# A mixture-of-experts kernel on one core: the matrix of routing weights made by VectorE from lists along the free axis

## The reference

```python
lg = (hf @ w_rg + b_rg)                       # 8 group logits per token
grp = jnp.argmax(lg, axis=-1)                 # one group of 8
le_sel = ...                                  # the 8 expert logits of that group
top_v, top_j = lax.top_k(le_sel, 2)           # two experts of it
wts = pg_top * jax.nn.softmax(top_v, axis=-1)
...
def expert_block(args):
    xb, e = args
    return (jax.nn.silu(xb @ w_g[e]) * (xb @ w_u[e])) @ w_d[e]
...
yb = yb * row_w[:, None]
out = jnp.zeros((N, D)).at[row_tok].add(yb)
```

## Time and profile before

| | us |
|---|---|
| median of 3 runs | 1274.16 (1273.81 to 1274.68) |
| the profiled execution | 1274.61 |
| its span, first to last instruction | 1272.5 |
| PE busy | 1164.9 (92%) |
| VectorE busy | 465.5 (37%) |
| ScalarE busy | 311.8 (25%) |
| HBM read | 406.22 MB, 321 GB/s over the span |

### The profile page before, as it was taken

How to read it: one execution, slowest core, us unless ns; L and a number is a source line. 1 busy time by engine, 2 the same in 40 slices (tenths; PEclk the granted TensorE clock), 3 DMA queues, 4 the chain that set the end, 5 groups by cost and what they waited for, 6 DMA issues and landing times.

```text
span 1272.5 us, 34338 instructions
## 1 busy us (share of the span) xinstructions
PE 1164.9 (92%) x14651; PEld 737.1 (58%) x14652; DVE 465.5 (37%) x1045; ACT 311.8 (25%) x752; POOL 142.9 (11%) x84
## 2 busy tenths in 40 slices
PE   5999999989998998789999999999999978897786
PEld 4878777768874554445555555555555544454443
DVE  3799443444344232132233333223332212322123
ACT  4133234384221121111122111112211211121112
POOL 2454444166000000000000000000000000000000
PEclk9999999999998999899999999999999989998898
DMA  6332111254067999997999999999999999999993
GB/s 234 124 113 89 67 66 67 67 199 171 28 272 313 422 424 427 427 425 329 418 424 427 424 424 425 394 427 427 425 424 427 422 426 428 423 427 426 423 424 120
DMA packets 51306, 408.79 MB, mean 321 GB/s; under 512 B 6410, under 2 KB 6567, under 8 KB 21066
## 3 DMA queue, kind: packets, MB, share of 16 engines
q1 hardware_dynamic: 50778, 407.22, 77.4%
q0 software_dynamic: 352, 1.06, 0.3%
q10 hardware_dynamic: 144, 0.07, 0.0%
HBM read 406.22 MB, written 2.11 MB: 321 GB/s over the span
## 4 chain that ended last, share of the span: by engine, by line
PE 51%; DMA 41%; ACT 3%; DVE 3%; issue 1%; SPq 1%; DVEq 0%; ACTq 0%
DMA sb_weights<-in_w_exp_up 40%; PE ps_pair_a L1688 10%; PE ps_pair_a L1444 9%; PE ps_pair_b L1749 4%; PE ps_pair_a L1669 4%; PE ps_scores L1701 4%; PE ps_pair_b L1444 4%; PE ps_scores L1740 2%; PE ps_pair_a L1676 1%; DMA sb_consts<-in_consts 1%; ACT sb_late L946 1%; PE ps_pair_a L1495 1%; PE ps_pair_b L1495 1%; PE ps_scores L1509 1%; PE ps_pair_a L1619 1%
## 5 line engine op out<-in xcount | busy, mean ns | idle before, releaser
L1688 PE MATMUL ps_pair_a<-sb_weights,sb_late 128*32 128x256 f32 x4608 | 296.1, 410 | 52.9 <-DMA sb_weights<-in_w_exp_up 51.5
L1688 PEld LDWEIGHTS ps_pair_a<-sb_weights,sb_late 128*32 128x32 f32 x4608 | 163.9, 114 | 175.8 <-issue 86.1
L1365 DVE TENSOR_TENSOR sb_late<-sb_late,ps_pair_a 128x128 f32<-128x128 f32 x72 | 20.7, 287 | 522.0 <-ACT sb_late L954 522.0
L1669 PE MATMUL ps_pair_a<-sb_hT,sb_late 128*32 128x256 f32 x2336 | 140.2, 380 | 0.6 <-DVE sb_late L1238 0.6
L1701 PE MATMUL ps_scores<-sb_weights,sb_late 128*32 128x256 f32 x2304 | 138.7, 382 | 0.0
L1669 PEld LDWEIGHTS ps_pair_a<-sb_hT,sb_late 128*32 128x32 f32 x2336 | 75.0, 109 | 63.5 <-issue 17.4
L954 ACT ACTIVATE sb_late<-ps_pair_a 128x128 f32<-128x128 f32 x72 | 20.0, 277 | 312.5 <-PE ps_pair_a L1688 312.5
L1701 PEld LDWEIGHTS ps_scores<-sb_weights,sb_late 128*32 128x32 f32 x2304 | 73.9, 111 | 37.9 <-issue 1.4
L1360 DVE TENSOR_TENSOR sb_x<-sb_x,ps_pair_b 128x512 f32<-128x512 f32 x94 | 60.4, 684 | 95.4 <-PE ps_pair_c L1749 95.4
L1749 PE MATMUL ps_pair_b<-sb_g_ffn,sb_late 32*128 32x512 f32 x376 | 88.4, 587 | 0.0
L1749 PE MATMUL ps_pair_c<-sb_g_ffn,sb_late 32*128 32x512 f32 x376 | 88.4, 587 | 0.0
(11 more groups left out here) (396 smaller groups left out, 1376.0 us busy)
## 6 DMA issues: line engine op xcount, KB each, us to landing
sb_weights<-in_w_exp_up SPq DMA_DIRECT2D x59, 2048.0 KB, 14.6
sb_weights<-in_w_exp_down SPq DMA_DIRECT2D x59, 2048.0 KB, 14.5
sb_weights<-in_w_exp_gate SPq DMA_DIRECT2D x59, 2048.0 KB, 14.5
sb_ring<-in_w_in SPq DMA_DIRECT2D x9, 2048.0 KB, 8.9
sb_x<-in_x SPq DMA_DIRECT2D x8, 512.0 KB, 5.2
sb_ring<-in_w_conv_pw SPq DMA_DIRECT2D x1, 2048.0 KB, 9.1
sb_ring<-in_w_attn_up SPq DMA_DIRECT2D x1, 2048.0 KB, 8.0
sb_ring<-in_w_out SPq DMA_DIRECT2D x1, 2048.0 KB, 13.0
```

Source lines behind the costliest of these rows:

```text
L1365: dve.tensor_tensor(act, gsig, ps_gu[:, P:2 * P], ALU.mult).then_inc(act_ready, 1)
L1669: last = mm(ps_rows[g * BLK:(g + 1) * BLK, 0:QCOLS], onehots[c][:, t, :], h2[:, t, g * QCOLS:(g + 1) * QCOLS], start=t == 0, stop=t == T - 1)
L1688: last = mm(ps_gu[g * BLK:(g + 1) * BLK, 0:2 * P].rearrange("p (a n) -> p a n", a=2), rows, weights[:, at:at + 3:2, r % 4, cols], start=r ...
```

## The change

The weighted matrix is made in another way. The lists `dest` and `wts` (two values for each token) are put along the free axis once, in the lead: VectorE multiplies each with the identity (`spread`), PE sums it over the partitions by a product with ones (`spread_rows`, after the `down` of position 1), so that every partition holds the list of 512 tokens, and ACT copies the four results of 128x512 to SBUF (`d_list`, `w_list`). Then for each position VectorE compares the list of slots with the slot number of the partition (`slot_at`), multiplies with the list of weights, does so for both choices and adds them (`weigh_slots`). One intermediate result lies in the PSUM bank that `share_rows` wrote before. `share_rows`, its copy on ACT, and the multiplication and addition of `shares` are gone, those of the lead too.

Moved with this: `place_rows` follows `take_loads` directly; `weigh_choices` comes after `next_onehot(0, 0)`; the three `weigh_slots` of the lead come after `next_onehot(1, 1)`; ACT copies the lists between its work for positions 1 and 2. The table of constants has another order and one more column.

```diff
@@ scalar, position()
-                act_e.wait_ge(w_done, p + 1)
-                act_e.activation(w_rows[c], ps_w, ACT.Copy).then_inc(w_ready, 1)
...
-            for p in range(LEAD):
-                position(p, p)
+            position(0, 0)
+            position(1, 1)
+            for done, banks, rows in ((d_done, ps_d, d_list), (w_done, ps_w, w_list)):
+                for k in range(2):
+                    act_e.wait_ge(done, k + 1)
+                    act_e.activation(rows[:, k, :], banks[:, k, :], ACT.Copy).then_inc(list_ready, 1)
+            position(2, 2)
@@ vector
+            def spread(rows, values, made):
+                for k in range(2):
+                    one = values.rearrange("p (t k) -> p t k", k=2)[:, :, k]
+                    dve.tensor_tensor(rows[:, k, :].rearrange("p (t s) -> p t s", t=T), over(one, P),
+                                      ident.unsqueeze(1).to_broadcast([P, T, P]), ALU.mult).then_inc(made, 1)
...
-                dve.wait_ge(hot_b, n + LEAD + 1)
-                dve.tensor_tensor(hot_k, hot_k, over(wts, BLK), ALU.mult).then_inc(loop_v, 1)
-                dve.wait_ge(loop_v, 3 * n + 4)
-                dve.tensor_tensor(shares[c], onehot2[:, :, 0, :], onehot2[:, :, 1, :], ALU.add).then_inc(hot_w, 1)
+            def weigh_slots(p, c):
+                dve.wait_ge(loop_w, 3 * p + 1)
+                dve.wait_ge(w_ready, p + 1)
+                dve.scalar_tensor_tensor(out=w_rows[c], in0=d_list[:, 0, :], scalar=slot_at, in1=w_list[:, 0, :],
+                                         op0=ALU.is_equal, op1=ALU.mult).then_inc(loop_w, 1)
+                dve.scalar_tensor_tensor(out=ps_second, in0=d_list[:, 1, :], scalar=slot_at, in1=w_list[:, 1, :],
+                                         op0=ALU.is_equal, op1=ALU.mult).then_inc(loop_w, 1)
+                dve.wait_ge(loop_w, 3 * p + 3)
+                dve.tensor_tensor(w_rows[c], w_rows[c], ps_second, ALU.add).then_inc(w_ready, 1)
+                dve.tensor_scalar(slot_at, slot_at, float(BLK), None, ALU.add).then_inc(loop_w, 1)
...
-            weigh_choices()
-            static_shares()
-            for p in range(NBUF):
-                static_share(p)
             place_rows()
             gate_and_up(1)
+            dve.wait_ge(loop_v, 1)
+            spread(d_list, dest, d_spread)
+            dve.wait_ge(d_spread, 2)
             next_onehot(0, 0)
+            weigh_choices()
+            spread(w_list, wts, w_spread)
             gate_and_up(2)
             next_onehot(1, 1)
+            dve.wait_ge(list_ready, 4)
...
+            for p in range(LEAD):
+                weigh_slots(p, p)
...
                     if c == 0:
                         add_half(2 * r, 0, ps_add)
                         add_half(2 * r + 1, 1, ps_add)
+                    weigh_slots(p, c)
@@ tensor
-            def share_rows(p, c):
-                pe.wait_ge(hot_w, p + 1)
-                for t in range(T):
-                    for g in range(NG):
-                        last = mm(ps_w[g * BLK:(g + 1) * BLK, t * P:(t + 1) * P], shares[c][:, t, :], ident,
-                                  start=True, stop=True)
-                last.then_inc(w_done, 1)
+            def spread_rows():
+                for spread, done, banks, rows in ((d_spread, d_done, ps_d, d_list), (w_spread, w_done, ps_w, w_list)):
+                    for k in range(2):
+                        pe.wait_ge(spread, k + 1)
+                        mm(banks[:, k, :], ones, rows[:, k, :], start=True, stop=True).then_inc(done, 1)
...
-                    pe.wait_ge(w_ready, NBUF * n)
+                    pe.wait_ge(w_ready, NBUF * n + 1)
@@ tensor, lead()
-                share_rows(p, p)
                 down(p, p, p + 1)
+                if p == 1:
+                    spread_rows()
```

More of the change, by code:

```diff
@@ L79 @@
 _at = 0
-for _n, _w in [("ident", P), ("before", P), ("ones", P), ("pos", BLK), ("block", MAXPOS),
-               ("flip", P), ("lane8", EPG), ("mask", P),
-               ("turn", MAXPOS), ("class_before", NE), ("class_of", NBUF), ("class", 1), ("base", 1), ("expert", 1),
-               ("blocks_min", 1), ("movable", 1), ("tie_row", NE), ("tie", 1), ("opposite", 1), ("pos_static", BLK),
-               ("bucket", 5 * P)]:
+for _n, _w in [("ident", P), ("ones", P), ("pos", BLK), ("slot", 1), ("bucket", 5 * P), ("before", P), ("block", MAXPOS),
+               ("flip", P), ("lane8", EPG), ("mask", P), ("turn", MAXPOS), ("class_before", NE), ("class_of", NBUF),
+               ("class", 1), ("base", 1), ("expert", 1), ("blocks_min", 1), ("movable", 1), ("tie_row", NE), ("tie", 1),
+               ("opposite", 1), ("pos_static", BLK)]:
     CONST[_n] = (_at, _w)
@@ L119, in constants @@
     put("pos", np.tile(np.arange(BLK), (P, 1)))
+    put("slot", p % BLK - BLK * LEAD)
     put("block", np.tile(np.arange(MAXPOS), (P, 1)))
@@ L355, in block_kernel @@
         y_sb = [working(QCOLS) for _ in range(NBUF)]
-        shares = [working(T * BLK).rearrange("p (t s) -> p t s", t=T) for _ in range(NBUF)]
         w_rows = [router_w[:, 0:SEQ], g_ffn[:, 0:SEQ], g_ffn[:, SEQ:2 * SEQ]]
         g_fin = weights[:, 0, 0:2, :].rearrange("p a n -> p (a n)")
+        BUCKET = CONST["bucket"][0]
+        NTABLE = MAXPOS + 3 * NE + 2
+        w_list = consts[:, BUCKET + NTABLE:BUCKET + NTABLE + 2 * SEQ].rearrange("p (k s) -> p k s", k=2)
+        assert BUCKET + NTABLE + 2 * SEQ <= CONST["tie_row"][0]
+        slot_at = const("slot")
+        d_list = late[:, late_at[0]:late_at[0] + 2 * SEQ].rearrange("p (k s) -> p k s", k=2)
+        assert late_at[0] + 2 * SEQ <= LATE
         def h2T(t):
@@ L392, in block_kernel @@
         ps_rows, ps_hTb = bank[1], bank[1][:, QCOLS:]
-        ps_y, ps_w = ps_s[:, 0, :], ps_s[:, 1, :]
+        ps_y, ps_second = ps_s[:, 0, :], ps_s[:, 1, :]
+        ps_d, ps_w = pair_b, pair_c
         ps_tables, ps_ranks, ps_loads = ps_oT, ps_o, ps_t[:, 2 * P:]
         ps_add = [bank[2], ps_t, ps_o, ps_oT]
-        ps_last = [bank[0], bank[1], ps_y, ps_w]
+        ps_last = [bank[0], bank[1], ps_y, ps_second]
         pairs = [pair_a, ps_s, pair_b, pair_c]
@@ L449, in block_kernel @@
         xT_done, xT_ready = sem("xT_done"), sem("xT_ready")
-        hot_w, w_done, w_ready = sem("hot_w"), sem("w_done"), sem("w_ready")
+        d_spread, d_done, w_spread, w_done, list_ready = (sem("d_spread"), sem("d_done"), sem("w_spread"), sem("w_done"),
+                                                          sem("list_ready"))
+        w_ready, loop_w = sem("w_ready"), sem("loop_w")
         sums_begun, sums_done, sums_added = sem("sums_begun"), sem("sums_done"), sem("sums_added")
@@ L484, in small_temp @@
             return split_view(cols(math.prod(shape))[0:rows], shape)
-        static_at, static_w, static_w2 = small_temp(T, NBUF), small_temp(T, NBUF), small_temp(T, NBUF)
+        static_at = small_temp(T, NBUF)
         g_e, hot_g, hot_1, hot_2, le = (small_temp(T, EPG) for _ in range(5))
@@ L494, in block_kernel @@
         steps = hot_c.rearrange("p t e -> p (t e)")[:, 0:2 * T * (SEQ // BLK)].rearrange("p (j n) -> p j n", j=2 * T)
-        tables = consts[0:1, CONST["bucket"][0]:CONST["bucket"][0] + MAXPOS + 3 * NE + 2].bitcast(I32)
+        tables = consts[0:1, BUCKET:BUCKET + NTABLE].bitcast(I32)
         loads_at = tables[:, 0:MAXPOS]
@@ L1340, in _ @@
             hot_k = onehot2.rearrange("p t k s -> p (t k) s")
             def next_onehot(c, n):
-                dve.wait_ge(loop_v, 3 * n + 1)
-                dve.wait_ge(hot_w, n + LEAD)
+                dve.wait_ge(loop_v, 2 * n + 1)
+                dve.wait_ge(hot_b, n + LEAD)
                 dve.tensor_tensor(hot_k, over(dest, BLK), pos8, ALU.is_equal).then_inc(loop_v, 1)
-                dve.wait_ge(loop_v, 3 * n + 2)
+                dve.wait_ge(loop_v, 2 * n + 2)
                 dve.tensor_tensor(onehots[c], onehot2[:, :, 0, :], onehot2[:, :, 1, :], ALU.add).then_inc(hot_b, 1)
@@ L1782, in _ @@
             pe.wait_ge(listed, 1)
-            pe.wait_ge(loop_v, 1)
+            pe.wait_ge(list_ready, 4)
             pe.sem_inc(sums_done, 1)
@@ L1797, in _ @@
                         sum_round(r, 1, ps_add)
-                    share_rows(p, c)
                     down(p, c, loads)
```

10 lines of the change are left out of this document (2 added, 8 removed).

## The result

The changed kernel takes 1265.97 us (1264.67 to 1268.09, 4 runs) against 1273.99 (1273.66 to 1274.68) for the kernel before: the ratio is 0.9938, with a 95% interval of 0.9925 to 0.995. The profiled execution took 1266.51 (span 1264.7), 8.1 us less than the profiled one of before. That is 0.6%, well over the 0.2% that can be told from no change, and 1.0 us from the forecast of 1265.0.

The account below looks back on a forecast made before the run. The prediction took expert-weight transfers to bound the loop, so PE's time counts only where DMA stood idle; 4.5 + 3.7 + 1.0 = 9.2 us off 1274.16 gave 1265.0 us, own range 1262.5 to 1267.5, wider range 1259.5 to 1270.

Parts of the forecast that it names:

- the lead: Ahead of the loop: PE's wait and share_rows go, first refill comes earlier; 4.5 us, with ends 2.8 and 5.8.
- the loop: PE loses 0.89 us a position: 2.7 us at the hole near 596 us, 1.0 later; 3.7 us, ends 0 and 7.9.
- the end: Behind the last weights, share_rows leaves the chain that ended last; gain 1.0 us.
- A: Rival: the lead gives nothing, as spreading the lists delays the second refill; 1269.5 us, chance 0.17.
- B: Rival: both holes close, lead gain 5.8 us and the hole at 596 us gone, 7.9 us; 1259.5 us, chance 0.15.
- C: Rival: PE's time was hidden anyway in the lead and loop, only the end gains; 1273.2 us, chance 0.10.
- D: Rival: slower, as PE waits more in the loop and its clock drops, 1.6 us a place; 1277.8 with 8, chance 0.06.
- second hole: Idle transfers in the loop, 6.9 us from 596 to 606 us; forecast to lose 2.7 us, leaving 4.2.
- VectorE: hidden: In the loop, weigh_slots takes 2.35 us a position on VectorE, leaving 0.9 us idle in class 0; costed at nothing.

Follow-up runs that it names:

- e1: The kernel before, with VectorE running weigh_choices and the static shares ahead of the tables in the lead, every share_rows kept: 1269.98 us, ratio 0.9966.
- e3: The kernel before, with one product in place of the 16 of share_rows in each loop position, lead unchanged: 1270.57 us, ratio 0.9966.
- e8: The kernel after, with position 1's gate and up products ahead of position 0's down, and four products on PE before the tables: 1265.03 us.
- e7: The kernel after, unchanged, measured again: 1266.81 us, ratio 0.9943 to the kernel before.
- e10: The kernel after, unchanged, measured once more: 1265.11 us, ratio 0.9927 to the kernel before.
- e9: The kernel after, with four products of 128x256 on PE in the lead ahead of its wait for the tables: 1265.81 us, ratio 0.9931.
- e5: The kernel after, with the gate and up products of position 1 put ahead of position 0's down in the lead: 1265.52 us, ratio 0.9927.
- e4: The kernel after, with four more products of 128x512 on VectorE in every weigh_slots: 1267.66 us, ratio 0.9945 to the kernel before.
- e2: The kernel after, with 16 products the size of share_rows put back into each loop position on PE: 1269.73 us, ratio 0.9959.
- e6: The kernel after, with 48 identity products on PE between the gate and up third waits in class 2 of the loop: 1269.74 us, ratio 0.9967.

## Why the prediction was right, step by step

The forecast was a gain of 9.2 us, 4.5 in the lead, 3.7 in the loop and 1.0 at the end; the traces give 4.1, 3.2 and 0.5, together 7.8. In the loop and at the end the mechanism was right and the size a little too large; in the lead PE's path moved as forecast, but another wait ended last. None of the rivals came about: A is excluded by the 3.4 us left of the 7.2 us hole (and e1 and e3 show lead and loop separately), B by the 4.9 us left of the second, C by both, and D by the time.

**The lead: 4.1 for 4.5.** Order of time, PE in the lead of the kernel after (compare):

```profile
390.89 0.70 PE L1756 MATMUL ps_pair_b<-sb_late,sb_small 64*1 64x162 f32 x2
391.52 3.08 PE L1724 MATMUL ps_scores<-sb_weights,sb_late 128*32 128x256 f32 x32
394.43 3.82 PE L1711 MATMUL ps_pair_a<-sb_weights,sb_late 128*32 128x256 f32 x64
...
402.71 1.98 PE L1763 MATMUL ps_pair_b<-sb_late,sb_consts 128*128 128x512 f32 x4
404.53 1.88 PE L1763 MATMUL ps_pair_c<-sb_consts 128*128 128x512 f32 x4
406.34 3.86 PE L1711 MATMUL ps_pair_a<-sb_weights,sb_late 128*32 128x256 f32 x64
```

`down` follows the tables and the products of position 1 start at 394.43 (394.1 was forecast). The four products of `spread_rows` end at 406.3, where 405.8 was forecast, and the next refill goes out at 410.52. SP waits 4.4 us for the products behind the lists, but the one ahead is still landing (DMA share 1.01 from 405 to 425 us), so the lists cost nothing. What was mis-sized is the sentence "The refill can't start before the DMA drains at about 396.3". The bound is not the end of the flow but the landing of the gate third, as the chain of waits of the kernel after has it:

```profile
383.69 14.71 DMA sb_weights<-in_w_exp_gate
...
398.69 0.37 SPq L604
```

PE was done at 398.3, just as late by chance, but in e8 at 395.5 with the same refill. That the refill came near the 398 forecast is therefore partly luck, and from 396 to 404 us 3.2 us of idle transfers are left (share 0.60) where 2 were forecast. So an end of the range for the lead (5.8 us with the clock up, by its own terms 5.7) was not to be had: e7 and e10 had the clock up, and the refill at 398.28.

**The loop: 3.2 for 3.7.** The chain of the second hole was to lose three `share_rows` of 0.89 us, 2.7 in all. Order of time, PE in the kernel after (compare):

```profile
560.48 5.75 PE L1711 MATMUL ps_pair_a<-sb_weights,sb_late 128*32 128x256 f32 x64 [5.96 <-DMA sb_weights<-in_w_exp_up]
...
592.89 3.82 PE L1711 MATMUL ps_pair_a<-sb_weights,sb_late 128*32 128x256 f32 x64
```

From the start of the first to the end of the second it takes 596.7 - 560.5 = 36.2 us, before 603.19 - 564.68 = 38.5. The 2.3 us are the 2.7 less 0.4: PE came to the chain earlier, waited 5.96 instead of 4.22 us and then took 5.75 instead of 5.47 us for these products, and the `down` behind them was 0.07 us longer. That is rival D's mechanism; its price at this place is 0.4 us, since SP no longer waits for most of the later products. The later places gave 2.2 us where 1.0 was forecast, because the 7.9 us of the loop were not "nearly all" one hole: in the table above the loads run 1.3 us ahead up to the hole, the hole costs 7.0, which leaves a lag of 5.7, and the later losses are 2.2. The term that the prediction didn't have is the 1.5 us between the 14th and the 17th load. The chain of the kernel after, around it:

```profile
609.63 14.57 DMA sb_weights<-in_w_exp_up
...
624.42 16.03 DMA sb_weights<-in_w_exp_up
```

One third took 16.03 us to land, with the DMA engines full (share 1.01, 425 GB/s from 619 to 646 us). e7, the same kernel, has such a load too, but at another place (15.69 us, from 1186 us on), and e9 has one at 760 us; e10 has none. So it belongs to no step of the kernel. Each time one transfer of the queue that the profile lists as "instruction" begins within that load, at 633, 1199 and 766 us. The DMA view of the kernel after from 633 to 636 us has it (packets, MB, share of 16 engines):

```profile
q8 instruction: 1, 0.02, 2.3%
```

These three kernels have one such transfer each from 600 to 1230 us, and e10 has none. So it goes with the lost time, but one ahead of the hole (e5, at 530 us) cost nothing, and no run moves it: that it is the cause is likely and not shown. Without the slow load the loop would have given 4.7, as in e10. That 3.2 came near 3.7 is thus partly luck: 0.4 too little at the hole, 1.2 more at the later places, and 1.5 not foreseen.

**VectorE: hidden, as forecast.** Order of time, one `weigh_slots` in class 0 and the product behind it:

```profile
430.27 0.74 DVE L1363 SCALAR_TENSOR_TENSOR sb_router_w<-sb_late,sb_consts 128x512 f32<-128x512 f32 x1
430.94 0.75 DVE L1365 SCALAR_TENSOR_TENSOR ps_scores<-sb_late,sb_consts 128x512 f32<-128x512 f32 x1
431.73 0.69 DVE L1368 TENSOR_TENSOR sb_router_w<-sb_router_w,ps_scores 128x512 f32<-128x512 f32 x1
432.33 0.15 DVE L1369 TENSOR_SCALAR sb_consts<-sb_consts 128x1 f32<-128x1 f32 x1
433.69 0.29 DVE L1381 TENSOR_TENSOR sb_late<-sb_late,ps_pair_a 128x128 f32<-128x128 f32 x1 [1.21 <-ACT sb_late L964]
```

The four durations sum to 2.33 us (forecast 2.35), and 1.21 us of idle time are left ahead of the product (forecast 0.9, before 4.19). Busy time rose by 103.7 us, not 115. (Had each large instruction taken 1.1 us, the product would have come 0.2 us late, not 0.1 as the prediction has it.) That this margin isn't sharp either is shown by e4: with four more products there PE waits in 21 places, and no time was lost that can be told from none.

**The end: 0.5 for 1.0.** The chain that ended last, in the kernel after:

```profile
1232.18 6.08 PE ps_pair_a L1711 x64
...
1243.57 0.70 PE ps_pair_b L1770 x2
...
1255.51 0.45 issue
```

And in the kernel before:

```profile
1239.48 6.22 PE ps_pair_a L1688 x63
...
1251.80 0.70 PE ps_pair_b L1749 x2
```

From the start of the last gate and up products to that of the last sum it is 11.39 us, before 12.32: 0.93 less, with the 1.01 of `share_rows` gone. The 0.45 us in which VectorE waited for nothing that the profile shows, ahead of the final norm, were 0.04 in the kernel before. e2, e7 and e10 have it and e4 hasn't. In the traces that have it a transfer of an instruction queue (q14) begins 1.1 to 1.3 us after its start, and in e4 and the kernel before there is none; which brings which stays open.

The kernel after spreads over 1262.9 to 1268.1 us in its three measurements. Its last gate and up products took 6.08, 6.01 and 5.05 us in the three profiles, and the slow load cost 1.5, 1.1 and 0 us; in both e10 is the shortest, as it is in time. That makes up part of the spread, and the rest isn't explained.

## What to carry to other kernels

Where transfers set the time, look up the few places at which they stood idle and price an edit there alone: 47 us less work on PE and 104 us more on VectorE came to 8 us, most of it from two such places (4.1 and 2.3 us). A wait removed lets the next one show at once, here the landing of the transfer ahead of the same kind, so ask of each idle stretch what else the waiting queue wants before it may go on. Moving work ahead of a wait can be worth as much as removing it: e1 got the lead's whole gain with every product of the old method still in place.

## What the runs showed of the hardware that was not expected

A transfer's end is later for the queue that waits for it than the flow suggests. The transfer rate of the kernel after from 380 to 400 us, in slices of 0.5 us:

```profile
GB/s 426 426 393 492 459 360 393 393 459 459 393 377 393 393 459 344 442 442 393 442 410 442 492 442 459 410 426 328 393 492 459 229 131 98 98 0 0 33 0 393
```

The rate falls from 395.5 us on, three slices carry about 100 GB/s, and nothing of note shows after 397.5. But the DMA view from 397.5 to 398.5 us still counts three packets:

```profile
DMA packets 3, 0.00 MB, mean 0 GB/s; under 512 B 3, under 2 KB 3, under 8 KB 3
```

Narrower views put them between 397.8 and 398.0, with 16 such packets in all from 395.5 to 398.5, and SP is released at 398.40. So of the 2.9 us behind the fall of the rate some 2.5 are a tail in which little still moves, and 0.4 lie behind the last packet. Three transfers of the instruction queues (two of q8, one of q14) begin from 380 to 398 us as well; whether they make the tail isn't shown. The Trainium skill, "DMA: Bandwidth & Descriptors", section "Anatomy of one DMA — SWDGE (gpsimd) path", puts most of a transfer's fixed 2 us into the confirmation that the last byte has landed; it says so for another kind of queue. The trace leaves 0.4 us for it here.

After a wait for weights the same 64 products took 5.43 to 6.00 us instead of 3.82 in all four chains shown (e6, the kernel before, e3 and the kernel after), and the order of the waits (2.09, 4.22, 5.27 and 5.96 us) is not that of the durations (5.43, 5.47, 6.00 and 5.75): the length of the last wait alone doesn't set the price. The durations go with the granted clock, which is 0.68, 0.68, 0.59 and 0.63 while they run, a mean between the two levels of 1.2 GHz (0.5) and 2.4 GHz (1.00). At the end of e6, after a wait of 2.07 us, they took 3.85, at full clock. Table by stretch, the products of e3 and those at the end of e6:

```profile
565.00:570.80 5.80, 5.76 (x64) 3.09 (x68) 0.00 (x0) 0.00 (x0) 0.00 (x0) 0.59 1.04 436
...
1237.70:1241.50 3.80, 3.80 (x68) 2.18 (x72) 0.00 (x0) 0.00 (x0) 0.00 (x0) 1.00 1.01 418
```

The Trainium skill, "TensorE: Matmul & The Clock Gate", section "HAM oscillation — how this bites in real kernels", has a piece behind a DMA wait begin cold, that is, at the lower level; the rows agree but for that last one. The time shows that it decides little in a kernel that the transfers bound: e6 has the higher mean clock in its profiled execution (0.978 for 0.958) and is 2.9 us slower than e7.
